# A two-group mixer layer on one core: m stored once as fp32 and split into two fp16 parts at the output projection

## The chip, the cores and the metric

One core of one Trainium2 chip. The metric is the device time of one execution in microseconds, lower is better.

## What is computed

One layer over 4096 prompt tokens and 8 x 16 sample tokens, width 1024:

```
h = rms_norm(x, norm_pre)
p = h @ w_in                      # 1024 x 3728: GLA, token-shifted RWKV and gate columns
o_gla  = gated linear attention (4 heads of 128), RMSNorm per head, * g_norm * silu(z_g)
o_rwkv = RWKV-7 delta rule (8 heads of 64), GroupNorm, + bonus, * silu(z_r)
m = concat([o_gla, o_rwkv])       # 512 + 512 columns per token
y = x + rms_norm(m @ w_out, norm_post)
```

The states and the last shifted row are outputs too. The matmuls with w_in and w_out need nearly fp32 precision: both factors are held as two fp16 parts (high and low), and three products are summed (high x high, low x high, high x low).

## The kernel before, in words

Tokens lie in 33 tiles of 128 (tile 0 holds the sample streams) and 17 blocks: block 0 is tile 0, blocks 1 to 16 have 256 tokens, two tiles each. There are two phases, one after the other, each with a program of its own for every engine.

**First phase, `gla_phase`.** A list of steps per block, `a_steps`, is run by all engines; each takes the steps that it has a function for. For each tile: `take_o` (ScalarE, L928) reads the outputs from PSUM, `squares` (TensorE) and `rnorm` (ScalarE) make the norm, `gate` (VectorE, L1111) multiplies by it (L1114) and by the gate (L1117). Then `high_m` (ScalarE, L948; the copy is L952) makes the fp16 high part in `m_hl`, `low_m` (VectorE, L1120; the subtraction is L1122) the low part, and `put_mg` (SP, L556; the store is L560) writes both to the scratch tensor `mg` in HBM. `take_o` of the next tile waits for `low_m`, since it overwrites `o_sb`. The last store and two others count into `tail_out`, for which the second phase waits.

**Second phase, `rwkv_phase`.** The order of each engine within a block is written out by hand: `PE_BODY`, `ACT_BODY`, `DVE_BODY`, `SP_BODY`. Names with `-` belong to the block before. The y of a tile is kept by `keep_y` in one of two slots of `yT`, normalised (`centred`, `deviation`, `normed`), scaled and shifted by `affine` (L2300), given the bonus (L2586) and gated (L2589) by `gated`. Then `high` (ScalarE, L2307), `low` (VectorE, L2593) and `put_m` (SP, L1639) split and store it as in the first phase, into the scratch tensor `mr`. `keep_y` of the tile two later waits for `low`.

**The output projection** has two sources of order. Per tile and half of w_out's columns TensorE runs 24 matmuls of 128x128 by 128x512 (`project_out`, all recorded at L1855), cut into six units of 4: 12 units a tile. In the bodies of the last two blocks and one more, where no more input projections are left, each of their places ("room") takes one unit: 108 units, 9 tiles. The other 24 tiles follow one after another, the tail. What the other engines do for a tile is put in a list with a due position in units (`out_jobs`); at a point `out` in the hand-written order an engine takes over all jobs that are due by then, and in the tail all in order of their positions. For tile t: `fetch` (SP) at 12t - 8, `o_squares` (ScalarE, L2326, Square with a sum) and `o_scaled` (VectorE, L2609) at 12t + 6 and 12t + 12, `o_sum` and `o_rstd` (L2331 to L2336) at 12t + 13, `o_done` (VectorE, L2624) at 12t + 15.6, `put_y` (SP, L1721) at 12t + 15.7.

`fetch` waits until tile t - 2 has been multiplied, loads the GLA half of m (L1709) and the RWKV half (L1711) into `m_c`, which has two slots, and x (L1714) into `x_c`, after the y of tile t - 2 has been stored from there. TensorE waits for the two m loads. For tile 0 `fetch` also loads norm_post. w_out comes in 16 parts of 128x512 (`get_ow`, SP, L1694), which `ow_high` (L2315) and `ow_low` (L2598) split; they are placed at points of blocks 14 and 15.

All queues are in order: an instruction that waits holds everything behind it on its engine.

Of the kernel before, what the change touches and what calls it, by code (L numbers as in the profile page):

```python
# [14 lines left out]

# [12 lines left out]
P = 128  # L28
# [36 lines left out]
def build(nc, t):  # L65
    with ExitStack() as ctx:
# [18 lines left out]
        c["d_full"] = Count(ctx.enter_context(nc.semaphore("r_d_full")), "d_full", 1, len(ROUND_NO))  # L85
        setup(nc, t, c)
# [105 lines left out]
def a_steps(b):  # L192
# [64 lines left out]
    if b == LAST:  # L257
# [15 lines left out]
        def own_mean(i):  # L273
            steps.extend((j, own[i]) for j in ("squares", "rnorm", "gate", "high_m", "low_m", "put_mg"))
# [23 lines left out]
        steps.extend((j, own[1]) for j in ("high_m", "low_m", "put_mg"))  # L298
# [52 lines left out]
def gla_phase(nc, t, c):  # L351
# [8 lines left out]
    with ExitStack() as ctx:  # L360
# [51 lines left out]
        m_hl = sb("m_hl", [P, 2, 4, P], F16)  # L412
# [86 lines left out]
        mh_ok = sig("m_high", 1, NT)  # L499
        ml_ok = sig("m_low", 1, NT)  # L500
# [24 lines left out]
        def _(sp):  # L525
# [30 lines left out]
            def put_mg(tile):  # L556
                b, i = home_of(tile)
# [254 lines left out]
        def _(act):  # L812
# [134 lines left out]

            def high_m(tile):  # L948
                act.wait_ge(m_ok.sem, m_ok.at(tile, 2))
                if tile:  # L950
                    act.wait_ge(mg_out.sem, mg_out.at(tile - 1, 1))
                act.activation(m_hl[:, 0], o_sb[:, :, :], ACT.Copy).then_inc(*mh_ok.up(tile))  # L952
# [9 lines left out]
            def split_w2(n):  # L962
# [7 lines left out]
                    "rnorm": rnorm, "high_m": high_m, "split_w2": split_w2,  # L970
# [13 lines left out]
        def _(dve):  # L984
# [126 lines left out]
            def gate(tile):  # L1111
                b, i = home_of(tile)
                dve.wait_ge(r_ok.sem, r_ok.at(tile, 2))
                dve.scalar_tensor_tensor(out=o_sb[:, :, :], in0=o_sb[:, :, :], scalar=g_norm[:, 0:1],  # L1114
                                         in1=o_sq[:, :, :], op0=ALU.mult, op1=ALU.mult).then_inc(*m_ok.up(tile))
                dve.wait_ge(m_ok.sem, m_ok.at(tile, 1))
                dve.tensor_tensor(o_sb[:, :, :], o_sb[:, :, :], zg[:, b % 2, :, columns(tile)],  # L1117
                                  ALU.mult).then_inc(*m_ok.up(tile))

            def low_m(tile):  # L1120
                dve.wait_ge(mh_ok.sem, mh_ok.at(tile, 1))
                dve.tensor_tensor(m_hl[:, 1], o_sb[:, :, :], m_hl[:, 0], ALU.subtract).then_inc(*ml_ok.up(tile))  # L1122
# [14 lines left out]
            def split_w2(n):  # L1137
# [9 lines left out]
                    "gate": gate, "low_m": low_m, "split_w2": split_w2,  # L1147
# [47 lines left out]
    join_e:2 affine:0 squares:2 out gamma taken:x0 odd:2 turned:3 high:0 rnorm:0 out rnorm:1 z1:3 join_e:3  # L1195
    keep_y:2 taken:x2 centred:1 out taken:x8 odd:3 turned:4 out deviation:1 affine:1 z1:4 join_e:4 keep_y:3
    high:1 out
""".split()
DVE_BODY = """
    zc:0 masked:1 -mixed:x10 -low:1 even:0 keep_w:1 mixed:x12 -bonus:0 out -r -bonus:1 next:0 join_o:1 mixed:x4  # L1200
    out masked:2 zc:1 decay out even:1 keep_w:2 normed:0 next:1 mixed:x6 join_o:2 gated:0 out masked:3 zc:2
    clamp:0 even:2 mixed:x0 keep_w:3 clamp:1 low:0 out unit:0 unit:1 next:2 join_o:3 k_prime mixed:x2 out
# [12 lines left out]
POST = ("centre", "variance", "centred", "deviation", "high", "normed", "affine", "gated", "low", "get_gate", "put_m")  # L1215
OUT_FROM = LAST - 1
OW_FROM = -6
OW_AT = [0, 0, 1, 1, 2, 2, 3, 3, 4, 4, 4, 5, 5, 5, 6, 6]
# [61 lines left out]

def out_jobs():
# [6 lines left out]
    for tile in range(NT):  # L1288
        p = 12.0 * tile
        put(max(p - 8.0, 0.0), "fetch", tile)  # L1290
# [21 lines left out]
def pe_program():  # L1312
# [3 lines left out]
    for part in [opening_jobs(PE_BODY)] + [body_jobs(PE_BODY, b) for b in range(NB + 1)]:  # L1316
        jobs = []
        for job, arg in part:
            if job == "room":
                jobs.append(("out", next(units)))  # L1320
# [10 lines left out]
def side_program(table, mine):  # L1331
# [4 lines left out]
    for b in range(NB + 1):  # L1336
        jobs = []
        for job, arg in body_jobs(table, b):
# [9 lines left out]
            for j, at in (("get_ow", OW_FROM), ("ow_high", OW_FROM + 1), ("ow_low", OW_FROM + 1)):  # L1348
                if j in mine:
                    jobs += [(j, k) for k in range(2 * KT) if OW_AT[k] + at == arg]  # L1350
            if "fetch" not in mine:
# [29 lines left out]
def rwkv_phase(nc, t, c):  # L1381
# [9 lines left out]
    mr_d = nc.dram_tensor("scratch_mr", (NT, P, 2, 4, P), F16, kind="Internal").ap()  # L1391
# [3 lines left out]
    with ExitStack() as ctx:  # L1395
# [55 lines left out]
        m_hl = sb("m_hl", [P, 2, 4, P], F16)  # L1451
# [20 lines left out]
        def Ss(j):  # L1472
# [5 lines left out]
                  m_hl[:, :, :, :].rearrange("p w g t -> p (w g t)").bitcast(F32))]  # L1478
# [8 lines left out]
        o_junk = [xb[:, 2 * h:2 * h + 2].rearrange("p c g t -> p (c g t)") for h in range(2)]  # L1487
# [47 lines left out]
        mr_out = sig("mr_out", 1, NT, 16)  # L1535
# [6 lines left out]
        ss_in = sig("ss_in", 8, 1, 16)  # L1542
# [4 lines left out]
        mc_in = [sig("mc_in0", 2, 17, 16), sig("mc_in1", 2, 16, 16)]  # L1547
# [5 lines left out]
        set_ok = sig("pool_set", SET_ALL, 1)  # L1553
# [20 lines left out]
        ones_ok = sig("ones", 1, 1)  # L1574
# [34 lines left out]
        mh_ok = sig("m_high", 1, NT)  # L1609
        ml_ok = sig("m_low", 1, NT)  # L1610
# [15 lines left out]
        def _(sp):  # L1626
# [75 lines left out]
            def fetch(tile):  # L1702
                b, i = home_of(tile)
                slot, n = tile % 2, tile // 2
                if tile == 0:
                    sp.wait_ge(y_full.sem, y_full.at(last_chunk(LAST - 2), 1))
                if tile >= 2:
# [996 lines left out]
```

## Time and profile before

| | us |
|---|---|
| median of 3 runs | 2375.19 (2369.25 to 2376.35) |
| span of the profiled execution, first to last instruction | 2370.8 |
| TensorE matmul busy | 2287.6 (96%) |
| ScalarE busy | 1427.8 (60%) |
| VectorE busy | 1308.5 (55%) |
| GpSimd busy | 569.9 (24%) |
| granted TensorE clock, mean | 0.994 |

The page gives the profiled execution's span and no time of its own around it; the span lies 4.4 us under the median of the runs. PE is TensorE, PEld its weight load, ACT ScalarE, DVE VectorE, POOL GpSimd, SP SyncE, of which only the issue of transfers is shown (SPq). A releaser is what an engine's idle time ended with. Matmuls are pipelined, so their durations overlap. PEclk is the granted clock as a share of full speed.

### The profile page before, as it was taken

How to read it: one execution, taken by the hardware profiler on the slowest of the kernel's cores; microseconds unless marked ns; L12 is line 12 of the kernel's file. 1: busy time of each engine (PE TensorE's matmuls, PEld its weight loads, DVE VectorE, ACT ScalarE, POOL GpSimd, SP SyncE). 2: the span in 40 equal slices, each digit the busy share in tenths (PEclk: the TensorE clock that was granted, in tenths of full speed). 3: DMA queues.
4: the chain of work that ended last, by engine and by line, in shares of the span. 5: the costliest groups of instructions: out<-in, count | busy, mean ns of one | idle time of the engine just before them, and what ended most of it. 6: DMA issues, size and time to landing. Idle time of an engine off the chain costs nothing. (4 is left out here: it accounts for less than half of the span.)

```text
span 2370.8 us, 72009 instructions
## 1 busy us (share of the span) xinstructions
PE 2287.6 (96%) x31129; PEld 1721.6 (73%) x31129; DVE 1308.5 (55%) x2477; ACT 1427.8 (60%) x2820; POOL 569.9 (24%) x1070
## 2 busy tenths in 40 slices
PE   6999999999999998889999999999999998999998
PEld 5777777777777766778888887888888874544443
DVE  6444444444444443566777776767777775432222
ACT  8466666666666645546776666666676774543323
POOL 0000000000000001155555554455555555000000
PEclk9999999999999998999999999999999999999999
DMA  7112222222211111123222222222222234354453
GB/s 244 67 55 73 73 73 69 69 81 91 73 54 54 54 63 48 43 52 78 76 71 73 69 67 76 76 76 76 76 67 74 56 93 145 115 167 150 152 160 125
DMA packets 198779, 204.74 MB, mean 86 GB/s; under 512 B 108608, under 2 KB 151936, under 8 KB 194112
## 3 DMA queue, kind: packets, MB, share of 16 engines
q1 hardware_dynamic: 196304, 184.41, 26.3%
q10 hardware_dynamic: 2160, 15.73, 1.8%
q8 instruction: 247, 4.05, 0.7%
q14 instruction: 68, 0.56, 0.1%
HBM read 119.81 MB, written 80.28 MB: 84 GB/s over the span
## 5 line engine op out<-in xcount | busy, mean ns | idle before, releaser
L675 PE MATMUL d<-h,w_hi 128*128 128x256 f16 (+1 forms) x3264 | 527.4, 270 | 9.8 <-DVE w_lo L1133 8.1
L675 PE MATMUL d<-h,w_lo 128*128 128x256 f16 (+1 forms) x1632 | 436.7, 270 | 0.0
L1816 POOL TENSOR_TENSOR r_inv_tmp<-r_inv 64x30 f32<-64x30 f32 (+14 forms) x480 | 259.5, 541 | 435.0 <-DMA r_inv<-scratch_blocks 398.7
L675 PEld LDWEIGHTS d<-h,w_hi 128*128 128x128 f16 x3264 | 315.1, 98 | 55.6 <-issue 14.9
L1855 PE MATMUL r_d<-h,w_hi 128*128 128x256 f16 (+1 forms) x1824 | 297.0, 269 | 0.8 <-DVE carry_s L2394 0.8
L1818 POOL TENSOR_TENSOR r_inv<-r_inv,r_inv_tmp 64x30 f32<-64x30 f32 (+14 forms) x480 | 278.2, 580 | 37.6
L1855 PE MATMUL first<-h,w_hi 128*128 128x256 f16 x1664 | 282.5, 273 | 0.0
L1855 PE MATMUL r_d<-h,w_lo 128*128 128x256 f16 (+1 forms) x912 | 241.6, 269 | 0.0
L1855 PE MATMUL first<-h,w_lo 128*128 128x256 f16 x832 | 227.2, 273 | 0.1
L1759 POOL MEMSET r_run_s<- 128x128 f16 x1 | 0.2, 204 | 930.6 <-POOLq L360 930.6
L1855 PEld LDWEIGHTS r_d<-h,w_hi 128*128 128x128 f16 x1824 | 171.9, 98 | 37.2 <-issue 14.7
L1855 PEld LDWEIGHTS first<-h,w_hi 128*128 128x128 f16 x1664 | 159.2, 98 | 33.9 <-issue 12.9
L675 PEld LDWEIGHTS d<-h,w_lo 128*128 128x128 f16 x1632 | 160.4, 98 | 17.5
L1855 PE MATMUL r_d<-w_hi,r_ops 128*128 128x512 f16 x560 | 167.0, 379 | 0.2 <-DMA r_ops<-scratch_mr 0.2
L675 PE MATMUL d<-w_hi,h 128*128 128x512 f16 x528 | 157.0, 379 | 2.0 <-DVE w_lo L1133 2.0
L1855 PE MATMUL first<-w_hi,r_ops 128*128 128x512 f16 x496 | 148.1, 380 | 0.0
L2168 ACT ACTIVATE r_praw<-r_carry 128x2 f32<-128x2 f32 (+1 forms) x112 | 22.5, 201 | 155.3 <-PE r_d L1855 77.5
L1855 PE MATMUL r_d<-w_lo,r_ops 128*128 128x512 f16 x280 | 106.2, 379 | 0.0
L1855 PEld LDWEIGHTS r_d<-w_hi,r_ops 128*128 128x128 f16 x560 | 53.9, 98 | 64.7 <-issue 1.5
L1114 DVE SCALAR_TENSOR_TENSOR o_sb<-o_sb,g_norm,o_sq 128x512 f32<-128x512 f32 x33 | 24.8, 751 | 137.4 <-ACT o_sq L946 137.4
L675 PE MATMUL d<-w_lo,h 128*128 128x512 f16 x264 | 100.1, 379 | 0.0
L1855 PEld LDWEIGHTS r_d<-h,w_lo 128*128 128x128 f16 x912 | 89.7, 98 | 10.0 <-issue 1.0
(323 smaller groups left out, 4792.3 us busy)
## 6 DMA issues: line engine op xcount, KB each, us to landing
h<-in_x SPq DMA_DIRECT2D x33, 512.0 KB, 3.8
r_ops<-in_x SPq DMA_DIRECT2D x33, 512.0 KB, 4.2
out_y<-r_ops SPq DMA_DIRECT2D x33, 512.0 KB, 2.9
scratch_hT<-h SPq DMA_DIRECT2D x16, 1024.0 KB, 7.0
h<-scratch_hT ACTq DMA_DIRECT2D x15, 1024.0 KB, 7.0
scratch_mg<-m_hl SPq DMA_DIRECT2D x33, 256.0 KB, 2.0
r_zr<-scratch_zr SPq DMA_DIRECT2D x33, 256.0 KB, 3.6
r_bon<-scratch_bonus SPq DMA_DIRECT2D x33, 256.0 KB, 4.7
```

The source lines that it names most:

```text
L675: mm = pe.matmul(out, lhs(k, a, w), rhs(k, a, w), start=(n == 0), stop=(n == len(terms) - 1))
L1114: dve.scalar_tensor_tensor(out=o_sb[:, :, :], in0=o_sb[:, :, :], scalar=g_norm[:, 0:1], in1=o_sq[:, :, :], op0=ALU.mult, op1=ALU.mult).the ...
L1759: pool.memset(m[:, :], v).then_inc(*set_ok.up(0))
L1816: step(pool.tensor_tensor(tmp, inv[0:n, 0:u, u:u + 1].to_broadcast([n, u, w]), inv[0:n, u:u + 1, u + 1:32].to_broadcast([n, u, w]), ALU.mult))
L1818: step(pool.tensor_tensor(inv[0:n, 0:u, u + 1:32], inv[0:n, 0:u, u + 1:32], tmp, ALU.add))
L1855: mm = pe.matmul(out, lhs(k, a, w), rhs(k, a, w), start=(m == 0), stop=(m == 3 * KT - 1))
L2168: act.activation(praw[:, x % 2, 0:ng, 0], carry[:, g0:g0 + ng], ACT.Copy)
```

## The change

m of both groups is stored once, as fp32, in the new scratch tensor `m_d`. `high_m`, `low_m`, `high` and `low` and their places in the orders go. Instead the output projection loads both halves of a tile as fp32 (`get_m`) into one buffer each, `m_fp`: `m_f`, in the place of `m_hl`, and `up`, free after the last low-rank product; ScalarE copies both to fp16 (`m_high`), and VectorE subtracts (`m_low`), into `m_c`. TensorE waits for `m_low`. `m_fp` has one slot: `get_m` of a tile waits for `m_low` of the tile before. `get_m(0)` has a point of its own, four points before the projection begins. Some semaphores are merged or renamed to make room.

```diff
-            steps.extend((j, back[i]) for j in ("squares", "rnorm", "gate", "high_m", "low_m", "put_mg"))
+            steps.extend((j, back[i]) for j in ("squares", "rnorm", "gate", "put_mg"))
...
             def put_mg(tile):
-                sp.wait_ge(ml_ok.sem, ml_ok.at(tile, 1))
+                sp.wait_ge(m_ok.sem, m_ok.at(tile, 2))
-                sp.dma_start(t["mg"][b][:, i], m_hl[:, :, :, :]).then_inc(*stored)
+                sp.dma_start(c["m_d"][tile][:, 0], o_sb[:, :, :]).then_inc(*stored)
...
             def take_o(tile):
-                    act.wait_ge(ml_ok.sem, ml_ok.at(tile - 1, 1))
+                    act.wait_ge(mg_out.sem, mg_out.at(tile - 1, 1))
...
+M_FROM = -4
...
     for tile in range(NT):
         p = 12.0 * tile
+        if tile:
+            put(p - 8.0, "get_m", tile)
+        put(max(p - 5.0, 0.0), "m_high", tile)
+        put(max(p - 5.0, 0.0), "m_low", tile)
         put(max(p - 8.0, 0.0), "fetch", tile)
...
             def put_m(tile):
-                sp.wait_ge(ml_ok.sem, ml_ok.at(tile, 1))
-                sp.dma_start(mr_d[tile], m_hl[:, :, :, :]).then_inc(*mr_out.up(tile))
+                sp.wait_ge(post_ok.sem, post_ok.at(tile, 7))
+                sp.dma_start(m_d[tile][:, 1], yT[:, tile % 2]).then_inc(*mr_out[tile % 2].up(tile // 2))
...
+            def get_m(tile):
+                if tile:
+                    sp.wait_ge(ml_ok.sem, ml_ok.at(tile - 1, 2))
+                else:
+                    sp.wait_ge(d_full.sem, d_full.at(ROUND_NO[LAST, "la2"], 1))
+                sp.dma_start(m_fp[0], m_d[tile][:, 0]).then_inc(*ss_in.up(8 + 2 * tile))
+                sp.wait_ge(mr_out[tile % 2].sem, mr_out[tile % 2].at(tile // 2, 1))
+                sp.dma_start(m_fp[1], m_d[tile][:, 1]).then_inc(*ss_in.up(9 + 2 * tile))
...
-                if tile >= 2:
-                    sp.wait_ge(d_full.sem, d_full.at(ROUND_NO["out", tile - 2, 1], 1))
-                sp.dma_start(m_c[:, slot, 0], t["mg"][b][:, i]).then_inc(*mc_in[slot].up(n))
-                sp.wait_ge(mr_out.sem, mr_out.at(tile, 1))
-                sp.dma_start(m_c[:, slot, 1], mr_d[tile]).then_inc(*mc_in[slot].up(n))
...
             def project_out(arg):
-                    pe.wait_ge(mc_in[tile % 2].sem, mc_in[tile % 2].at(tile // 2, 2))
+                    pe.wait_ge(ml_ok.sem, ml_ok.at(tile, 2))
...
             def keep_y(q):
-                    act.wait_ge(ml_ok.sem, ml_ok.at(tile - 2, 1))
+                    act.wait_ge(mr_out[tile % 2].sem, mr_out[tile % 2].at(tile // 2 - 1, 1))
...
+            def m_high(tile):
+                if tile == 0:
+                    act.wait_ge(y_full.sem, y_full.at(last_chunk(LAST - 2), 1))
+                if tile >= 2:
+                    act.wait_ge(d_full.sem, d_full.at(ROUND_NO["out", tile - 2, 1], 1))
+                act.wait_ge(ss_in.sem, ss_in.at(8 + 2 * tile + 1, 1))
+                for a in range(2):
+                    act.activation(m_c[:, tile % 2, a, 0], m_fp[a], ACT.Copy).then_inc(*mh_ok.up(tile))
...
             def out_squares(arg):
+                if h:
+                    act.wait_ge(os_ok.sem, os_ok.at(tile, 1))
-                act.activation(o_junk[h], bank_of(("out", tile, h))[:, :], ACT.Square,
+                act.activation(o_junk, bank_of(("out", tile, h))[:, :], ACT.Square,
...
+            def m_low(tile):
+                for a in range(2):
+                    dve.wait_ge(mh_ok.sem, mh_ok.at(tile, a + 1))
+                    dve.tensor_tensor(m_c[:, tile % 2, a, 1], m_fp[a], m_c[:, tile % 2, a, 0],
+                                      ALU.subtract).then_inc(*ml_ok.up(tile))
```

## Rows read from the trace of the kernel before

**Rows 1.** The page, busy time, share of the span and instructions
```profile
PE 2287.6 (96%) x31129; PEld 1721.6 (73%) x31129; DVE 1308.5 (55%) x2477; ACT 1427.8 (60%) x2820; POOL 569.9 (24%) x1070
```

**Rows 2.** Busy time by stretch: stretch, length, engines, PEclk, DMA share, GB/s
```profile
110.00:936.00 826.00, 818.78 (x6943) 633.71 (x6940) 369.76 (x715) 516.17 (x831) 0.00 (x0) 1.00 0.20 65
...
1100.00:1950.00 850.00, 840.74 (x17456) 698.24 (x17455) 624.42 (x1154) 592.29 (x1317) 453.43 (x816) 1.00 0.28 73
1950.00:2080.00 130.00, 115.93 (x2035) 68.96 (x2034) 68.65 (x131) 65.47 (x150) 34.96 (x61) 0.99 0.44 132
...
2125.00:2365.00 240.00, 237.87 (x1103) 107.63 (x1100) 66.63 (x117) 76.38 (x165) 0.00 (x0) 1.00 0.47 147
```

**Rows 3.** The chain in order of time, first and last whole tile: start, us, engine
```profile
2103.87 10.36 PE first L1855 x48
...
2352.51 10.37 PE first L1855 x48
```

**Rows 4.** Timeline of the first phase's end, by engine; last row: page, issues
```profile
910.88 0.38 ACT L936 ACTIVATE o_sq<-OB 128x256 f32<-128x256 f32 x1 [0.84 <-DVE m_hl L1122]
...
926.72 1.10 PE L788 MATMUL d<-o_sq,ones_dv 128*128 128x512 f32 x2 [1.67 <-ACT o_sb L937]
...
935.08 0.32 SPq L560 DMA_DIRECT2D scratch_mg<-m_hl  x1
...
scratch_mg<-m_hl SPq DMA_DIRECT2D x33, 256.0 KB, 2.0
```

**Rows 5.** Lines L2307 and L2593: ns min/median/max; idle of L2307 until
```profile
L2307 ACT ACTIVATE r_m_hl<-r_yT x33: 613/631/634, 1112.2 to 2096.1; 128x512 f16<-128x512 f32 x33
...
  DVE r_yT L2589: 23.0, 16
...
L2593 DVE TENSOR_TENSOR r_m_hl<-r_yT,r_m_hl x33: 677/691/908, 1112.9 to 2097.5; 128x512 f16<-128x512 f32 x33
```

**Rows 6.** Timeline where w_out is loaded, SP, ACT and PE
```profile
1962.44 1.42 SPq L1694 DMA_DIRECT2D h<-in_w_out  x3
...
1969.93 1.97 ACT L2315 ACTIVATE w_hi<-h 128x512 f16<-128x512 f32 x3 [5.27 <-DMA h<-in_w_out]
...
1976.34 0.46 PE L2033 MATMUL r_EO<-r_S,r_ops 64*64 64x64 f32 x16 [3.65 <-DVE r_S L2557]
```

**Rows 7.** Busy time by stretch, around the same place; last row: timeline, PE
```profile
1965.00:1970.00 5.00, 4.83 (x93) 3.08 (x94) 0.69 (x1) 0.07 (x1) 4.29 (x10) 1.00 1.00 325
...
1975.00:1980.00 5.00, 3.66 (x51) 2.05 (x52) 4.69 (x9) 3.44 (x7) 4.53 (x7) 0.77 0.67 159
...
1990.00:2000.00 10.00, 7.74 (x137) 4.20 (x130) 6.71 (x12) 4.77 (x12) 8.67 (x18) 1.00 0.13 49
...
1999.62 0.43 PE L1978 MATMUL r_EO<-r_TD,h 64*64 64x32 f32 x16 [2.26 <-DVE r_Zc L2530]
```

**Rows 8.** Tiles 6 to 8: timeline of DVE, ACT, SP, and the chain
```profile
2080.68 0.69 DVE L2589 TENSOR_TENSOR r_yT<-r_yT,r_zr 128x512 f32<-128x512 f32 x1
...
2082.18 5.29 PE r_d L1855 x24
...
2091.54 1.65 ACT L2300 ACTIVATE r_yT<-r_yT,lnb_s,sc 128x128 f32<-128x128 f32 x4 [0.76 <-DVE r_yT L2580]
...
2097.64 0.34 SPq L1721 DMA_DIRECT2D out_y<-r_ops  x1
```

**Rows 9.** Timeline of a tail tile, PE and SP
```profile
2196.95 0.59 PE L1855 MATMUL r_d<-w_hi,r_ops 128*128 128x512 f16 x2
...
2202.10 0.72 SPq L1711 DMA_DIRECT2D r_ops<-scratch_mr  x1
```

**Rows 10.** Tail loads of m: issue of L1709, ns min/median/max; landing of L1711
```profile
L1709 SPq DMA_DIRECT2D r_ops<-scratch_mg x24: 320/432/1477, 2108.4 to 2346.7; - x24
...
DMA to landing us min/median/max: 3.6/3.9/4.5
```

**Rows 11.** Timeline, three copies to fp16 in a row on ACT
```profile
1957.85 1.66 ACT L2315 ACTIVATE w_hi<-h 128x512 f16<-128x512 f32 x3
```

More of the change, by code:

```diff
@@ L16 @@
+import itertools
 from contextlib import ExitStack
@@ L273, in own_mean @@
         def own_mean(i):
-            steps.extend((j, own[i]) for j in ("squares", "rnorm", "gate", "high_m", "low_m", "put_mg"))
+            steps.extend((j, own[i]) for j in ("squares", "rnorm", "gate", "put_mg"))
         steps += [("get_h", 0), ("get_h", 1)]
@@ L297, in a_steps @@
         steps.append(("put_zr", b))
-        steps.extend((j, own[1]) for j in ("high_m", "low_m", "put_mg"))
+        steps.append(("put_mg", own[1]))
         return steps
@@ L1194 @@
     out tanh:la0 squares:0 tanh:lw2 tanh:la2 deviation:0 odd:1 out turned:2 k_factor taken:x6 z1:2 keep_y:1
[L1195 removed]
+    join_e:2 affine:0 squares:2 out gamma taken:x0 odd:2 turned:3 rnorm:0 out rnorm:1 z1:3 join_e:3
     keep_y:2 taken:x2 centred:1 out taken:x8 odd:3 turned:4 out deviation:1 affine:1 z1:4 join_e:4 keep_y:3
[L1197 removed]
+    out
 """.split()
 DVE_BODY = """
[L1200 removed]
+    zc:0 masked:1 -mixed:x10 even:0 keep_w:1 mixed:x12 -bonus:0 out -r -bonus:1 next:0 join_o:1 mixed:x4
     out masked:2 zc:1 decay out even:1 keep_w:2 normed:0 next:1 mixed:x6 join_o:2 gated:0 out masked:3 zc:2
[L1202 removed]
+    clamp:0 even:2 mixed:x0 keep_w:3 clamp:1 out unit:0 unit:1 next:2 join_o:3 k_prime mixed:x2 out
     -td masked:4 zc:3 beta a mixed:x8 strict:0 out strict:1 even:3 keep_w:4 normed:1 rkk next:3 join_o:4 gated:1
@@ L1214 @@
 AHEAD = ("scores", "inner", "turn", "solve", "join", "masked", "keep_w", "join_o", "turned", "z1", "join_e")
-POST = ("centre", "variance", "centred", "deviation", "high", "normed", "affine", "gated", "low", "get_gate", "put_m")
+POST = ("centre", "variance", "centred", "deviation", "normed", "affine", "gated", "get_gate", "put_m")
 OUT_FROM = LAST - 1
 OW_FROM = -6
+M_FROM = -4
 OW_AT = [0, 0, 1, 1, 2, 2, 3, 3, 4, 4, 4, 5, 5, 5, 6, 6]
@@ L1319, in pe_program @@
             if job == "room":
-                jobs.append(("out", next(units)))
+                jobs += [("out", u) for u in itertools.islice(units, 1)]
             elif job == "piece":
@@ L1350, in side_program @@
                     jobs += [(j, k) for k in range(2 * KT) if OW_AT[k] + at == arg]
+            if "get_m" in mine and arg == M_FROM:
+                jobs.append(("get_m", 0))
             if "fetch" not in mine:
@@ L1450, in rwkv_phase @@
         bon = sb("bon", [P, 4, P])
-        m_hl = sb("m_hl", [P, 2, 4, P], F16)
+        m_f = sb("m_f", [P, 4, P])
         st = sb("st", [P, 2, 4])
@@ L1486, in rwkv_phase @@
         npost = hT[:, LAST % 2].rearrange("p a k t -> p (a k t)")[:, 0:2 * D].bitcast(F32)
-        o_junk = [xb[:, 2 * h:2 * h + 2].rearrange("p c g t -> p (c g t)") for h in range(2)]
+        m_fp = [m_f[:, :, :], up[:, :].rearrange("p (g t) -> p g t", g=4)]
+        o_junk = lor[:, :].bitcast(BF16)
         wv_hi = w_hi[:, :].rearrange("p (k n) -> p k n", k=KT)
@@ L1608, in rwkv_phase @@
         post_ok = sig("post", 7, NT)
-        mh_ok = sig("m_high", 1, NT)
-        ml_ok = sig("m_low", 1, NT)
+        mh_ok = sig("m_high", 2, NT)
+        ml_ok = sig("m_low", 2, NT)
         ow_hi = sig("ow_high", 2 * KT, 1)
@@ L1833, in _, with released @@
             RELEASE.update({r: (carry_ok, k + 1) for k, r in enumerate(XROUNDS)})
+            def released(old):
+                if old[0] == "out":
+                    pe.wait_ge(ot_ok.sem, ot_ok.at(old[1], old[2] + 1))
+                elif old[0] == "centre":
+                    pe.wait_ge(yc_ok.sem, yc_ok.at(old[1], 2 * old[2] + 2))
+                elif old[0] == "variance":
+                    pe.wait_ge(post_ok.sem, post_ok.at(old[1], 1))
+                else:
+                    s, k = RELEASE[old[1]]
+                    pe.wait_ge(s.sem, s.at(old[0], k))
             def claim(key):
@@ L2319, in out_squares @@
                 act.wait_ge(d_full.sem, d_full.at(ROUND_NO["out", tile, h], 1))
-                if tile == 0 and h == 0:
-                    act.wait_ge(x_out.sem, x_out.at(LAST, 4))
                 if tile:
@@ L2339, in _ @@
                     "gamma": gamma, "load_h": lambda b: load_h(b + 2), "centred": centred, "deviation": deviation,
-                    "high": high_part, "affine": affine, "k_factor": k_factor, "ow_high": split_out, "o_squares": out_squares, "o_rstd": out_rstd,
+                    "m_high": m_high, "affine": affine, "k_factor": k_factor, "ow_high": split_out, "o_squares": out_squares, "o_rstd": out_rstd,
                     "odd": odd_unknowns, "keep_y": keep_y, "turned": keep_turned, "z1": keep_z1,
@@ L2627, in _ @@
             does = {"mixed": mixed, "decay": decay, "clamp": clamp, "unit": unit, "k_prime": k_prime, "rkk": rkk, "kappa": make_kappa, "r": make_r, "beta": make_beta, "a": make_a, "strict": strict,
-                    "bonus": bonuses, "normed": normed, "gated": gated, "low": low_part, "ow_low": split_out,
+                    "bonus": bonuses, "normed": normed, "gated": gated, "m_low": m_low, "ow_low": split_out,
                     "o_scaled": out_scaled, "o_sum": out_sum, "o_done": out_done, "zc": add_state,
```

75 lines of the change are left out of this document (23 added, 52 removed).

## The prediction, made before the changed kernel was run

> **What bounds the kernel now.** I read the page's busy times first: TensorE is busy for 2287.6 of 2370.8 us [rows 1]. The table of stretches says where the other 83 us lie: 7 in the first head group (110 to 936), 9 in the body of the second (1100 to 1950), 14 between 1950 and 2080, 2 in the tail; the rest is the start of either group, where the change moves nothing [rows 2]. The chain of waits ends in 25 links of 10.36 us, 48 matmuls each, from tile 8 (2103.87) to tile 32, with no other engine between them [rows 3]. So a freed operation of ScalarE or VectorE is worth at most the few idle us of its stretch, while every us by which a tail tile is late adds its full length. The sum is made against the span of 2370.8; the median of the runs shown is 2375.2, 4.4 more, and that distance is carried over.
>
> **First head group.** Per tile one copy on ScalarE and one subtraction on VectorE go (33 of each; their twins of the second group took 631 and 691 ns [rows 5]). SP stores the fp32 tile as soon as it is gated: as many bytes in rows as long. In exchange take_o now waits for the store to have landed, no longer for the subtraction. In the usual order four or five rounds lie between the two, so that costs nothing; only in the last block are they close. There the old wait ended at 910.88 [rows 4]; the gated tile is ready 1.4 us earlier, its store lands 2.0 us after issue [rows 4], so take_o comes 0.6 us later. Behind it on ScalarE are a table load and a tanh, and TensorE has a round to do meanwhile: nothing. For the last tile the order is friendlier: tanh of zr no longer stands behind a copy, and TensorE's wait of 1.67 us on o_sb shrinks by about 0.35 [rows 4]. At the hand-over SP issued the last store at 935.08, after the subtraction [rows 4]; without it the phase ends about 0.25 earlier. **Together -0.6** (bounds -1.2 and +0.5, the latter if take_o's 0.6 isn't covered).
>
> **Body of the second group.** Again one copy and one subtraction per tile go; the copy also held ScalarE for 1.4 us in 16 blocks, waiting for the gated tile [rows 5]. TensorE idles only 9.3 us in those 850 [rows 2], so the relief is worth between nothing and 3: **-1.0**. keep_y waits for the landed store two tiles back; that store now goes out right after get_gate's two loads, more than 10 us ahead: nothing. The new semaphores and the waits of o_squares on its own engine are order that the engine keeps anyway.
>
> **Where w_out is loaded.** SP issued tile 0's two m loads, x and norm_post, and behind them three parts of w_out at 1962.44; ScalarE waited 5.27 us for the part that it splits at 1969.93, and TensorE behind it 3.65 us for the state at 1976.34 [rows 6]. The DMA engines were full, at 325 GB/s [rows 7]. get_m(0) moves 30 us forward, past these on SP's queue: it stands between two jobs with idle time around it and takes two issues of 0.43 to 0.72 us [rows 9, 10]. So 0.52 MB leave a full queue: 1.6 us at 325 GB/s, 1.8 with the earlier issue. Against it m_low(0) puts 1.3 us of VectorE ahead of the masks and the state, which makes TensorE's next product late by about 1.2; this only moves into the 3.65 us wait behind it. The wait also cost clock: 0.77 of full speed in 1975 to 1980, where a wait of 2.26 us, in 1990 to 2000, left it at 1.00 [rows 7]. If the wait halves, some of that comes back; I take 0.8 of the 0.23 x 5 = 1.15 us. **Together -2.6** (bounds -5, both vanish; 0, the delay eats the gain).
>
> **Tiles 1 to 8 of the projection**, which lie between the last blocks. I placed each new job by its due time (loads 8 units ahead, the split 5; a unit is 4 matmuls). For tiles 1 to 5 the loads land and the split ends 1 to 5 us before TensorE gets there. Tile 6: VectorE comes to its subtractions after the gated tile (from 2080.68, 0.69 long), ends at about 2082.8, while TensorE began the tile at 2082.18 [rows 8]: **+0.6**. Tile 7 is just in time, but ScalarE and VectorE stand in its split until about 2093.8, in front of the last normalisation. So the affine step of 1.65 us, at 2091.54 before, comes at 2094.5, o_squares behind it about 2 us late, the y store of tile 6, at 2097.64 before [rows 8], about 2.6 late, and the loads of tile 8 stand behind that store: they land at 2105.0, the split ends at 2107.1, and TensorE wants it at 2104.5: **+2.6** (bounds 0 and 4).
>
> **The tail.** For one tile [rows 9]: TensorE starts it at 2196.95; the end of the tile before goes through Square, rstd and o_done to the y store; right behind it SP issues the m loads of the next tile, the second at 2202.10, 5.15 after the start. Landing takes 3.9 us in the median (3.6 to 4.5) [rows 10]: 9.05. The next tile starts at 10.36, so 1.3 us are spare. That place on SP stays the same: get_m stands at 12t - 8, put_y of two tiles before at 12t - 8.3. The x load follows as before. Now comes the split between landing and matmul. Copies follow each other at 0.52 ((1.66 - 0.63)/2 [rows 11, 5]), so the second ends 1.15 after the first's start; its subtraction takes 0.69; three hand-overs of 0.04 and a weight load of 0.1 make it **2.1 us against 1.3 spare: 0.8 late**. (Bounds: 1.8 for the split and 3.6 for landing give 0.2 late; 4.5 gives 1.4.) Readiness hangs on the end of the tile two before, not on the last. So when one tile waits 0.8, the next finds its data in time, and the one after waits again: a wait at every second tile, of the larger lateness of the pair, about 0.95. From tile 10 to 32 these are 12: **+11.4** (4 to 18). ScalarE's and VectorE's other tail work is not pushed: the split is over 0.1 us before o_squares is due. What is saved in TensorE's own work: nothing, the matmuls are the same.
>
> There is a lower price for a load in the Trainium skill, DMA: Bandwidth & Descriptors, whose section on the anatomy of one DMA fits 2.0 us and the bytes at 436 GB/s, for GpSimd's path; that would be 2.6 us for 256 KB, land the loads 1.3 earlier and leave no tail wait. The trace disagrees: no such load of the tail landed under 3.6 [rows 10], since a 512 KB store is issued ahead of it.
>
> **Sum**: -0.6 - 1.0 - 2.6 + 0.6 + 2.6 + 11.4 = **+10.4**: span 2381, time **2385.6**. What a measurement here can tell from no change is 0.3%, 7.1 us.
>
> **Rivals.**
> 1. The tail hides the split. It needs landing plus split in 5.2 us instead of 6.0: a load that lands in 3.1. For it: 1.3 us are spare, and the wait grows only from there. Against: the shortest landing is 3.6. It would leave -0.6 - 1.0 - 2.6 + 0.6 + 2.6, or with tile 8 hidden too -3.6: 2372 to 2374. 0.2, with the half way cases between this and mine.
> 2. Faster: the w_out stretch holds more than I give it. If the load's absence takes away the whole 3.65 and the clock's 1.15, and the body gives 3, with a hidden tail, it is 2375.2 - 0.6 - 3 - 4.8 = 2366.8. Both halves must come out; it decides at a tail lateness under 0.1. 0.06.
> 3. The tail's waits feed themselves: from 0.9 late on, m_high of one tile stands on ScalarE in front of o_squares of the tile before, its y store and thus the next loads come later. Each second wait then grows to 1.5 and the others no longer vanish: 18 to 22 in the tail instead of 11.4, 2392 to 2396. SP needed up to 1.48 instead of 0.43 us to issue a load [rows 10], which speaks for it; typical tiles stay 0.1 below. 0.14.
> 4. The waits cost clock, as in 1975 to 1980: 1.15 us at each of 12, 14 more, 2399. A wait of 2.26 us left the clock whole [rows 7], so 0.03. The Trainium skill, TensorE: Matmul & The Clock Gate, Part 1, says "the default state is throttled, and activity releases the throttle"; by that rule alone idle time is dangerous, and the long wait agrees, the short one doesn't show it.
>
> **How the numbers follow.** My case has 0.57, its own range being 2379 to 2392. The range 2375 to 2394 leaves out rival 2, rival 4, part of 1 and the top of 3. Slower by over 0.3% (above 2382.3): most of my case, rivals 3 and 4: 0.66. Within 0.3%: the low end of my case and most of rival 1: 0.27. Faster: 0.07.
>
> **What would show it.** In the changed profile: waits of TensorE on the subtraction of m_low at every second tail tile, near 0.8 to 1.0; links of 10.36 broken by them; the ScalarE copy idle on DMA m_f or up before it; SP's loads still behind the y store. One wait of 2 to 3 us at tile 8. ScalarE's wait for w_out near 3.5 and TensorE's on the state near 2, the clock above 0.77 there. SP's last store of the first group near 934.5, not 935.08. Wrong if the tail shows no waits, if they come at every tile, or if a block before 1950 loses TensorE time.

## The result, and the profile after

The changed kernel takes 2381.0 us (median of 18 runs, 2375.2 to 2387.7), the kernel before beside it 2372.0 (18 runs): a ratio of 1.0037, 95% interval 1.0027 to 1.0047. That is 8.8 us more, where the prediction had 10.4. (The ratios here are those on record; the quotient of the two medians can differ from them by up to 0.0006.) Applied to the 2375.2 on which the prediction stood, the ratio gives 2384.0, forecast 2385.6. The profiled execution has a span of 2380.2 us, 9.4 more than before.

The busy times by stretch, in the columns of [rows 2] (stretch, length, then PE, PEld, DVE, ACT, POOL, the granted clock, DMA share, GB/s):

```profile
110.00:936.00 826.00, 818.33 (x6923) 633.76 (x6951) 348.38 (x685) 496.83 (x801) 0.78 (x3) 1.00 0.20 66
1100.00:1950.00 850.00, 842.40 (x17520) 700.47 (x17518) 613.04 (x1137) 580.73 (x1297) 446.13 (x817) 1.00 0.28 74
1950.00:2080.00 130.00, 119.11 (x2027) 69.56 (x2026) 75.66 (x139) 72.54 (x165) 36.25 (x61) 0.97 0.44 132
2125.00:2365.00 240.00, 230.06 (x1058) 102.37 (x1057) 91.92 (x156) 96.48 (x198) 0.00 (x0) 1.00 0.46 145
```

Against [rows 2] TensorE is busier in the third stretch and idles 10 us in the last, where it idled 2. What it waits for from 2130 on (line, releaser, us in total, times, longest):

```profile
PE r_d L1858 <- DVE r_ops L2600: 8.4, 11, 1.1
PE first L1858 <- DVE r_ops L2600: 1.5, 1, 1.5
```

L2600 is the subtraction of m_low. These are twelve waits, at tile 11, at every second tile from there to tile 31, and at tile 32; tile 10 ahead of them waits 0.63. In the chain of waits (start, us, engine and line) the unbroken links of 10.36 [rows 3] are gone. Between the start of one tile that waited and that of the tile two behind it the chain now reads:

```profile
2198.36 10.54 PE r_d L1858 x48
2208.92 0.69 ACT r_lor L2332 x2
2209.62 1.28 ACT L2337
...
2211.57 1.43 DVE r_ops L2632 x2
2213.01 0.34 SPq L1722
...
2213.40 0.43 SPq L1702
...
2213.87 3.96 DMA up<-scratch_m
2217.87 0.04 issue
2217.91 0.64 ACT r_ops L2313
2218.58 0.55 DVE r_ops L2600
...
2219.19 0.70 DVE r_ops L2600
2219.89 0.14 issue
2220.02 10.54 PE r_d L1858 x48
```

The reader is to see the loop: the first tile's end, Square (L2332), rstd, o_done (L2632), the y store (L1722), behind it on SP the m loads (L1702), 3.96 us until they land, the split, and the tile after next. It closes in 2220.02 - 2198.36 = 21.66 us. Two tiles of TensorE's own work take 20.72, so 0.94 falls to each pair, as forecast (0.95): some 0.75 of waiting and 0.18 by which the link of the tile that waited is longer (10.54).

The longest wait, 1.51 us at tile 32, is not part of this pattern: it follows directly on a tile that waited. The second load of that tile took 5.57 us to land, where those of the tiles before it took 3.7 to 4.7:

```profile
2354.32 5.57 DMA up<-scratch_m
...
2362.08 10.53 PE first L1858 x48
```

Two other profiles with the loads in this place (the second buffer and tile 8 alone first, below) have no wait at tile 32.

The tiles ahead of the tail, TensorE's starts with the wait in brackets:

```profile
2076.36 0.59 PE L1858 MATMUL r_d<-w_hi,r_ops 128*128 128x512 f16 x2 [0.54 <-DVE r_ops L2600]
...
2100.72 0.59 PE L1858 MATMUL first<-w_hi,r_ops 128*128 128x512 f16 x2 [2.63 <-DVE r_ops L2600]
```

Tile 6 and tile 8 wait 0.54 and 2.63 (forecast 0.6 and 2.6).

To see the rest I compared start times of the same instructions. Profiles of one kernel differ by a few us in places, so the kernel before was profiled three times, and beside the changed kernel stand the experiments (described below) that have the stretch in question unchanged. Chunks are the 64-token steps of the recurrence, counted from 0. The table, in us:

| stretch | before | changed | difference | forecast |
|---|---|---|---|---|
| end of the first group, take_o of tile 29 to that of tile 32 | 50.0, 50.1, 50.0 | 46.2 or 46.3 in eight profiles, 44.7 in two | -3.8 (-5.3 in two) | -0.6 |
| from the second group's first product to its first product with the state | 93.5, 97.3, 96.0 | 96.0 to 98.0, mean 97.4 of ten | +1.8 | 0 |
| body, state product of chunk 0 to chunk 57 | 908.1, 903.3, 907.3 | 898.1 to 904.0, mean 901.4 of nine | -4.9 | -1.0 |
| w_out, chunk 57 to 61 | 71.2, 72.5, 69.6 | 67.1 to 70.4, mean 68.5 of seven | -2.6 | -2.6 |
| chunk 61 to the end of the last tile, which holds the waits of tiles 6 to 32 | 352.0, 351.8, 351.9 | 367.8 (its own profile) | +15.9 | +14.6 |

The first row is the surprise: it repeats to 0.1 us, and it is six times what was forecast. The reason stands in ScalarE's timeline. Before the change:

```profile
884.87 0.63 ACT L946 ACTIVATE o_sq<-o_sq 128x512 f32<-128x512 f32 x1
887.05 0.63 ACT L952 ACTIVATE m_hl<-o_sb 128x512 f16<-128x512 f32 x1 [1.55 <-DVE o_sb L1117]
887.70 1.28 ACT L884 ACT_TABLE_LOAD   x1
...
893.04 0.55 PE L753 MATMUL OB<-q_sb,Sd 64*128 64x128 f32 x1 [4.00 <-ACT k_tok L926]
```

and after it:

```profile
887.20 0.63 ACT L944 ACTIVATE o_sq<-o_sq 128x512 f32<-128x512 f32 x1
887.85 1.28 ACT L882 ACT_TABLE_LOAD   x1
...
893.20 0.34 PE L751 MATMUL OB<-q_sb,Sd 64*128 64x128 f32 x1 [1.82 <-ACT k_tok L924]
```

The copy `high_m` of tile 29 (L952) stood in the last block between that tile's rstd (L946) and the block's decay exponentials, which begin with the table load (L884). It waited 1.55 us for the gated tile and took 0.63: 2.18 us, by exactly which TensorE's wait on k_tok went from 4.00 to 1.82. The rest of the 3.8 is clock. TensorE's busy time and the granted clock (the column after the number of instructions) before, and after:

```profile
890.00:895.00 5.00, 1.96 (x11) 0.73 0.00 0
895.00:900.00 5.00, 5.00 (x31) 0.59 0.00 0
```

```profile
890.00:895.00 5.00, 3.18 (x22) 0.93 0.14 52
895.00:900.00 5.00, 5.00 (x37) 0.73 0.02 3
```

Before, (0.27 + 0.41) x 5 = 3.4 us of full clock are missing in the two slices, some 0.4 of it while TensorE still waited; afterwards (0.07 + 0.27) x 5 = 1.7. From the product that ended the wait (893.04 and 893.20) to take_o of tile 32 it took 32.32 us before and 30.77 after, so that 1.55 us came back behind the 2.18. In the two profiles with 44.7 the clock stayed at 1.00 throughout. Ahead of this place the copies were worth nothing: from take_o of tile 1 to that of tile 29 every profile of either kind takes the same 750 us to 0.1.

The second row of the table goes with the clock and not with the kernel. TensorE's busy time and granted clock, the kernel before in its first profile and in its second:

```profile
955.00:965.00 10.00, 6.52 (x122) 1.00 0.23 57
1005.00:1015.00 10.00, 6.93 (x160) 1.00 0.63 180
```

```profile
955.00:965.00 10.00, 6.53 (x95) 0.66 0.08 13
1005.00:1015.00 10.00, 6.93 (x156) 0.88 0.48 101
```

The first took 93.5 us, the second 97.3. The changed kernel has 1.00 and 0.66 there and took 96.2, the one with the early loads (first of the experiments) 0.66 and 0.83, and 97.8. Whether the change has a part in when the clock falls there is not shown.

The timelines at the other two places that the prediction named, the end of the first group (PE, SP) and the load of w_out (ACT), in the changed kernel:

```profile
925.32 1.10 PE L786 MATMUL d<-o_sq,ones_dv 128*128 128x512 f32 x2 [1.33 <-ACT o_sb L935]
...
933.45 0.43 SPq L558 DMA_DIRECT2D scratch_m<-o_sb  x1
...
1963.64 1.94 ACT L2321 ACTIVATE w_hi<-h 128x512 f16<-128x512 f32 x3 [0.81 <-DMA h<-in_w_out]
```

Against [rows 4, 6] the wait on o_sb is 0.34 shorter, the last store is issued 1.6 us earlier (933.45 for 935.08), and ScalarE's 5.27 us for w_out are 0.81. That last wait scatters: it is 3.4 to 5.3 us in the three profiles of the kernel before, and 0.55 to 3.0 in the nine with the w_out parts in their changed place and nothing added.

### The profile page after: what moved, and what is told of

It reads as the page before. It is cut to its first block and busy times, and to the rows that moved or that the text cites. A ratio compares the mean times of both kernels' runs of the same rounds, so it can differ in the third digit from the quotient of the medians.

```text
span 2380.2 us, 71977 instructions
## 1 busy us (share of the span) xinstructions
PE 2289.9 (96%) x31098; PEld 1722.2 (72%) x31129; DVE 1308.9 (55%) x2477; ACT 1426.0 (60%) x2820; POOL 562.3 (24%) x1070
```

## The experiments

**Loads of m ahead of the y store.** For the m loads of every tile, in out_jobs:

```diff
-            put(p - 8.0, "get_m", tile)
+            put(p - 8.5, "get_m", tile)
```

> The loads of m of a tile go on SP's queue ahead of the y store of the tile two before (due position 12t - 8.5 in place of 12t - 8); nothing else. My theory (the tail is late because the loads stand behind that store, 5.15 us after the tile's start, and the split follows them): the loads leave about 8 us earlier, so the 12 waits of the tail and the wait of 2.6 us at tile 8 go, 0.54 at tile 6 stays. That is 14 us less than the changed kernel: 0.998 of the kernel before. Rival, the split itself (two copies and two subtractions between load and matmul) or the single fp32 buffer sets the pace: the waits stay, 1.004. Rival, the waits cost nothing because the tail has other slack: 1.004 too.

2366.0 us, 0.9976 [0.9966, 0.9986] of the kernel before: by the ratios 5.7 us faster than it and 14.5 faster than the changed kernel (by the medians side by side 4.6 faster than the kernel before). The waits from tile 6 to 32 are a single one of 0.5 us (tile 6), where there were 15 of 13.8 in all, and the links are whole again:

```profile
PE r_d L1858 <- DVE r_ops L2600: 0.5, 1, 0.5
```

```profile
2209.70 10.36 PE r_d L1858 x48
2220.05 10.36 PE first L1858 x48
```

The first load of m of the tile that TensorE starts at 2220.05 now leaves here:

```profile
2207.19 0.32 SPq L1702 DMA_DIRECT2D r_m_f<-scratch_m  x1
```

That is 12.9 us ahead of its tile, where the changed kernel had 6.6 (2213.40 and 2220.02 in the chain above), so it leaves 6.2 us earlier and not the 8 that were expected. It goes out as soon as the last subtraction of the tile before has ended (2207.17): in this place the single buffer does set its time, at no cost.

So the tail's loss is the place of the loads on SP's queue, not the split as such. This version is faster than both kernels.

**The wait in two halves.** TensorE asks for the first half of the split at unit 0 of a tile and for the second at unit 3:

```diff
-                if n == 0:
-                    pe.wait_ge(ml_ok.sem, ml_ok.at(tile, 2))
+                if n in (0, 3):
+                    pe.wait_ge(ml_ok.sem, ml_ok.at(tile, 1 if n == 0 else 2))
```

> TensorE waits for the first subtraction of a tile before its first matmul and for the second one only before the fourth unit (the RWKV half of m is used from the 13th matmul on). The second subtraction ends 0.6 us after the first. My theory: lateness falls from about 0.85 to 0.25, so the 12 tail waits add up to about 3 instead of 10 us and tile 6's wait of 0.54 goes: 8 us less than the changed kernel, 1.000 to 1.001 of the kernel before. Rival, the waits come from a clock or a dispatch effect and not from the length of the split: nothing changes, 1.004.

2372.8 us, 1.0008 [0.9994, 1.0021]. In the tail the waits shrink to

```profile
PE r_d L1858 <- DVE r_ops L2600: 1.9, 5, 0.9
```

from 9.9 us in 12: one copy and subtraction less in front of TensorE is worth nearly the whole lateness. The wait at tile 8 stays (2.57 us), since there the load was late.

**A second buffer, same place on the queue.** From tile 11 on odd tiles load into memory of their own, so that get_m need not wait for the last subtraction of the tile before:

```diff
+        m_g = TT[:, 0].rearrange("p c g t -> p (c g t)")
...
-                if tile:
-                    sp.wait_ge(ml_ok.sem, ml_ok.at(tile - 1, 2))
+                if tile == 11:
+                    sp.wait_ge(u_full.sem, u_full.at(NQ - 1, 1))
+                elif tile:
+                    sp.wait_ge(ml_ok.sem, ml_ok.at(tile - (2 if tile > 11 else 1), 2))
```

> From tile 11 on odd tiles load m into a second pair of fp32 buffers, so get_m waits for the split of the tile two before, not of the last one; its place on SP behind the y store stays. My theory (SP's place sets the load's time, not the buffer): no change, waits at every second tail tile of 0.6 to 1.1 us, 1.004 of the kernel before. Rival, the single buffer: the waits go, 0.999 to 1.000.

2377.9 us, 1.0025 [1.0015, 1.0036], overlapping the changed kernel's interval. The tail's waits are the same:

```profile
PE r_d L1866 <- DVE r_ops L2608: 8.7, 11, 1.1
```

With the loads behind the y store, the one buffer is not what makes them late.

**Copies twice.** From tile 9 on ScalarE makes each copy of the split twice, the second behind the first:

```diff
                 for a in range(2):
+                    if tile > 8:
+                        act.activation(m_c[:, tile % 2, a, 0], m_fp[a], ACT.Copy).then_inc(*once_ok.up(tile - 9))
+                        act.wait_ge(once_ok.sem, once_ok.at(tile - 9, a + 1))
```

> The changed kernel (1.0037), with each of ScalarE's two copies of the split done twice, one after the other, for tiles 9 to 32: the split, 2.1 us so far, gets about 1.4 us longer. My theory (a tile waits at every second place for landing plus split minus the spare time): TensorE's wait goes from 0.95 to about 2.4 us per pair of tiles, 12 x 1.4 = 17 us in the tail, ratio 1.011. Rival 3 of the prediction, which begins where the copies come to stand in front of the Square of the tile before: that Square, its y store and the next loads come up to 1 us later, the second tile of the pair waits too, and the tail grows by 24 us or more, ratio 1.014 or over.

2399.0 us, 1.0114 [1.0098, 1.0131], 18 us over the changed kernel; 17 were expected by the simple sum. The pattern looks different:

```profile
2185.90 0.59 PE L1859 MATMUL r_d<-w_hi,r_ops 128*128 128x512 f16 x2 [1.24 <-DVE r_ops L2604]
...
2197.03 0.59 PE L1859 MATMUL first<-w_hi,r_ops 128*128 128x512 f16 x2 [0.61 <-DVE r_ops L2604]
...
2208.74 0.59 PE L1859 MATMUL r_d<-w_hi,r_ops 128*128 128x512 f16 x2 [1.20 <-DVE r_ops L2604]
...
2219.90 0.59 PE L1859 MATMUL first<-w_hi,r_ops 128*128 128x512 f16 x2 [0.63 <-DVE r_ops L2604]
```

Both tiles of a pair wait, 1.2 and 0.6 us. On ScalarE (its copies, then the Square of the tile before):

```profile
2205.40 0.63 ACT L2315 ACTIVATE r_ops<-r_m_f 128x512 f16<-128x512 f32 x1 [2.31 <-DMA up<-scratch_m]
...
2207.24 0.63 ACT L2317 ACTIVATE r_ops<-up 128x512 f16<-128x512 f32 x1
2207.78 0.58 ACT L2336 ACTIVATE r_lor<-first 128x512 bf16<-128x512 f32 x1
```

The Square at 2207.78 comes straight behind the last copy, with no idle time: it was held, as in rival 3. But its tile ended at 2197.03 + 10.53 = 2207.56, so it was held for 0.2 us only, and the pair doesn't show it. A pair takes 2208.74 - 2185.90 = 22.84 us, 1.18 more than the 21.66 of the changed kernel, and the split has grown by as much (from landing to the end of the second subtraction 3.3 us for 2.1). The Square that this pair's loop goes through wasn't held: it starts at 2196.46, 0.3 us after ScalarE was free. The second tile's wait is mostly the same lateness too: its data are ready 12.4 us after the end of the tile two before it, 0.2 of that by the hold, and the tile between covers 1.24 of waiting and 10.53 of work, which leaves 0.6. Twelve pairs at 1.18 make 14 us; the profile's tail is 16.3 longer than the changed kernel's, and 1.7 us of that is full clock missing after a wait of 2.35 us at 2138.49 (granted clock 0.90 and 0.75 in 2135 to 2145). So the simple sum holds up to this length of the split, and the 24 us or more of that rival do not come.

**Tile 7 alone first, tile 8 alone first.** The same edit of the place, for one tile each:

```diff
-            put(p - 8.0, "get_m", tile)
+            put(p - (8.5 if tile == 7 else 8.0), "get_m", tile)
```

> The changed kernel with one edit: the m loads of tile 7 alone are issued ahead of the y store of tile 5 instead of behind it. My theory for tile 8 (its split waits behind that of tile 7, the affine step and the y store of tile 6): the split of tile 7 ends earlier, the affine step is no longer pushed, and TensorE's wait at tile 8 falls from 2.63 us to about 0.9, what a tail tile waits anyway; the tail's 0.95 per two tiles stays. Rival: the wait at tile 8 comes from the load of tile 8 itself behind its own y store; then it stays at 2.6.

The wait at tile 8 fell to 2.06 us, not to 0.9: this expectation failed. ScalarE's first copy for tile 7 started straight behind the last normalisation's two operations, no longer waiting for the load, and was only 0.5 us earlier for it. What pushes the affine step is mostly the split's own time in front of it, not the lateness of its load.

> The changed kernel with the m loads of tile 8 alone ahead of the y store of tile 6. With the loads of tile 7 early, TensorE's wait at tile 8 only fell from 2.63 to 2.06 us. Theory now: what makes tile 8 late is the place of its own loads behind a y store that hangs on the affine step; which of its causes delays that step is secondary. Then the wait at tile 8 is gone here (0 to 0.3 us), and the tail's waits stay as in the changed kernel. Rival: the split of tile 8 itself stands behind the last normalisation on ScalarE and VectorE, so that a wait of 1 us or more is left at tile 8.

With `tile == 8` in that edit the wait at tile 8 is gone. The waits from tile 6 on are

```profile
PE r_d L1858 <- DVE r_ops L2600: 9.6, 13, 1.0
```

0.54 at tile 6 and twelve in the tail, from tile 9 on. So the loads' place behind the y store of tile 6 decides at tile 8 as in the tail. There is one profile of each; their times, 2377.8 and 2379.2, tell nothing apart.

**More in the queue where w_out is loaded.** A load of 512 KB that nobody needs, ahead of x of tile 0, as many bytes as the change takes out:

```diff
+                    sp.dma_start(x_c[:, 1, :], t["x"][1]).then_inc(*np_in.up(0))
```

> Just ahead of tile 0's x load, where the kernel before loaded m, SP issues one more load of 512 KB (x of tile 1, loaded again later), so that the parts of w_out stand behind as many bytes as before the change. My theory of the w_out stretch: ScalarE waits for w_out again as long as before (5 us), TensorE waits for the state 2 us more, and the product that meets the state of chunk 61 comes at 2007 or later where the changed kernel had 2004.8: 2 to 3 us more in the span up to there. Rival, the stretch got shorter because the copies and subtractions of the last blocks went away: no change there.

This expectation failed. ScalarE's wait for w_out is 2.9 us and not 5, which the kernel with the copies twice shows too (3.0), without that load. TensorE's wait on the state stays at 0.2, where the kernel before has 3.65, 3.0 and 2.1 in its three profiles and the other changed kernels 0.3 at most. Chunks 57 to 61 take 70.5 us against a mean of 68.5, and the kernel with the copies twice takes 70.4. So in this one profile the bytes in the queue do not bring the wait back, and the reason that the prediction gave for this stretch is not confirmed. The other candidate, the copies and subtractions of the last blocks that are gone, was not tried: the two runs that put old work back stop at tile 25.

**w_out ahead of x and norm_post**, on top of the early loads:

```diff
-            if "fetch" in mine:
-                jobs += late
             for j, at in (("get_ow", OW_FROM), ("ow_high", OW_FROM + 1), ("ow_low", OW_FROM + 1)):
...
-            if "fetch" not in mine:
-                jobs += late
+            jobs += late
```

> The kernel with the early loads (0.9976), and on SP's queue the parts of w_out due at a point go ahead of the x tile and norm_post due at the same point (1 MB that nobody needs before tile 0 ends). If full DMA queues in front of the w_out parts still cost TensorE time, ScalarE's wait of 2.0 us for a part goes and the stretch from 1940 to 2005 us gets 1 to 2 us shorter: 0.9970. Rival: what TensorE waits for there (2.9 us twice) hangs on the recurrence and not on w_out; then no change, 0.9976.

2365.6 us, 0.9981 [0.9967, 0.9995]: no change. ScalarE no longer waits for w_out at all, and TensorE waits in 1935 to 2015 as in the changed kernel (4.2 and 2.9 there):

```profile
PE r_EO L1978 <- DVE r_Zc L2533: 4.0, 2, 3.3
PE r_EO L1978 <- DVE h L2501: 2.8, 1, 2.8
```

What is left there hangs on the recurrence.

**The old work put back.** On top of the early loads, the second group's copy and subtraction at their old places into a spare buffer (tiles 0 to 25), then those of the first group too (all 33):

```diff
+            def high_again(tile):
+                if tile < 26:
+                    act.wait_ge(post_ok.sem, post_ok.at(tile, 7))
...
+                    act.activation(again[:, 0], yT[:, tile % 2], ACT.Copy).then_inc(*again_ok.up(tile))
```

> On top of the kernel with the early loads (0.9976 of the kernel before): the copy on ScalarE and the subtraction on VectorE of the second head group are put back at their old places for tiles 0 to 25, writing to a buffer that nobody reads; storing, loading and the tail stay as changed. The prediction gave this work 1.0 us in the body: 0.9980, the stretch between the first and the last state product before 1940 us grows by about 1. Rival: the body's relief is the part of the gain that I put too low, 3 to 5 us: 0.999 or over, TensorE's idle time in 1100 to 1935 rises from 3.4 us (mean of five profiles) back toward the 7.2 of the kernel before, and the stretch from 899 to 903 us back toward 908.

> As the run before, and the copy and subtraction of the first head group are put back too (all 33 tiles, with the wait of take_o on the subtraction; the store waits for it as before). The prediction gave both groups together 1.6 us: 0.9983. Rival with a body relief of 3 to 5 us: 0.9993 to 1.000. In either case the end of the first phase should fall back by 0.3 to 1.4 us, to near 938.0 for the first state products after it, where the changed kernel had 936.6.

The first gives 2366.6 us, 0.9984 [0.9974, 0.9994], both together 2369.2, 0.9996 [0.9985, 1.0007]. Against 0.9976 that is 1.9 and 4.7 us. The first interval holds both my 0.9980 and the rival's 0.999 and tells nothing apart; the second leaves out my 0.9983 and holds the rival's 0.9993 to 1.000. The body took 902.9 us in the first (mean without: 901.4) and 911.4 in the second, though the two kernels have the same body: it scatters by more than the effect. The first group does not scatter: with its copies back TensorE's wait on k_tok is back at its old length,

```profile
PE OB L754 <- ACT k_tok L927: 4.0, 1, 4.0
```

and its end takes 48.7 us instead of 46.2, which is 2.5 where 0.3 to 1.4 were expected (50.0 before, with more of the clock lost: here 0.77 and 0.89 in 895 to 905, 1.7 us of full clock). So the old work is what made the wait.

**The kernel before, twice more.**

> The kernel before, unchanged, for a second profile. If the body's relief of 5 to 10 us between the first and the last state product before 1940 us, which seven profiles without the copies show against one profile of the kernel before, is real, that stretch takes 908 us here too, and TensorE idles about 7 us in 1100 to 1935. If it is the scatter of one execution, the stretch takes 899 to 905 us, and idle time is near 3.4.

> The kernel before, unchanged, for a third profile, with the same expectations as the one ahead of it: 908 us and 7 us idle if the relief is real, 899 to 905 us and 3.4 if it is scatter. The first phase should end near 938.0 us in both, against a mean of 935.4 without the copies, if the 2.6 us there are real.

The body takes 903.3 and 907.3 us, TensorE idles 4.9 and 8.2 us in 1100 to 1935. One fits scatter, one the relief; with the first profile the mean is 906.3, 4.9 over the mean of the nine, and one of the three lies inside the range of the nine. The second group's first product starts at 938.7 and 938.6, as in the first profile (938.0), and at 934.1 to 937.0 in the ten with the first group changed. These are times from the start of the program, and the first group itself begins up to 3 us apart (take_o of tile 1 at 125.3 to 128.7), so the distances in the table are the better measure.

## Why the prediction was right, point by point

- **The tail** (+11.4): right in place, cause and size. 0.94 per pair in the chain, the loads behind the y store; moving them ahead removes it, a second buffer does not. The waits stand at tiles 10 and 11, at every second tile to 31, and at tile 32. The last, 1.51 us, was not in the sum and comes from one load that landed late (5.57 us).
- **One reason in it was wrong.** I put the 3.6 to 4.5 us of landing [rows 10] down to the 512 KB store issued ahead. With the loads ahead of that store they still took 3.0 to 4.1 (first, median 3.3 against 3.7) and 3.4 to 5.4 us (second, median 3.7 against 3.9). That no such load of the tail landed under 3.6 holds for the second loads; the first ones did from 3.5 on. The fit in the Trainium skill, DMA: Bandwidth & Descriptors, section on the anatomy of one DMA, which is for GpSimd's path and would give an estimate of 2.6 us, does not hold for these loads in either place (3.0 at least). The early place gains by starting 6.2 us sooner, and at most 0.4 by landing faster.
- **Tile 6 and tile 8** (+0.6, +2.6): measured 0.54 and 2.63. The chain to tile 8 was right in its last part (loads behind the y store, the y store behind the affine step); moving tile 7's loads gave back 0.57 of it, so its part about what pushes the affine step was wrong: the split's own time, not a late load.
- **First group** (-0.6): this step failed. It measured -3.8, and -2.5 with the copies put back and the same loss of clock. I looked at the wait on o_sb (1.67 [rows 4], now 1.33, the 0.35 forecast) and at the last store, and gave VectorE's and ScalarE's relief nothing else. The larger wait stood 33 us earlier, TensorE's 4.00 us on k_tok in the last block, and it was not in my rows. The copy waited 1.55 us there on its own account, so its removal was worth 2.18, and 1.55 us of clock came with it. take_o does wait for the store's landing now, as said (3.65 us at 910.45), and nothing waits for it.
- **Behind the hand-over** the second group's start gave back about 1.8 us of the gain, which I had at nothing. It goes with the granted clock at 955 to 965 and 1005 to 1015: the kernel before spans 93.5 to 97.3 us there by itself, and is back at 93.8, with a clock of 1.00 in both, in the run with both groups' copies. Why the clock falls more often with the first group changed is open.
- **The body** (-1.0, bounds 0 and 3): by the profiles -4.9, with a scatter of 5 to 6 us in either kernel. The medians of the early-load kernel are the other scale: it is 4.6 (medians side by side) to 5.7 us (ratio, interval 3.3 to 8.1) faster than the kernel before, 0.5 more without tile 6, for everything outside the tail, where I had 4.2. Of that the first group and the start of the second hold about 2.0 net and w_out 2.6, so that 0.5 to 1.6 are left for the body. So my 1.0 may have been too small, but neither scale decides it.
- **w_out** (-2.6): -2.6 on the mean, in part by luck. ScalarE's wait, which I had at 3.5, is 0.81 (0.55 to 3.0 over the profiles), and TensorE's wait of 3.65 us on the state, which I had at 2, is gone. Putting the bytes back did not bring it back, so that my reason for it is not shown. Of the clock nothing came back: 0.73 in 1960 to 1965 after the change, where 0.77 stood in 1975 to 1980 [rows 7], and 0.84 and 0.82 in 1990 to 2000, where it was 1.00. And the waits on Z and h in 1935 to 2015 grew from 5.2 to 7.1 us in all, the next limit.
- **The sum**: +10.4 forecast, 8.8 measured. The gains were larger than I had them, 5.1 to 6.2 us by the medians (9.5 by the means of the table) for 4.2. The loss from tile 6 on was 15.9 by the start times, 1.3 over the 14.6 forecast, about what tile 32's late load cost; the run with more in the queue, whose projection is the same, lost 13.5 there. So the tail carries the forecast by its mechanism, and that the rest came out near -4.2 is luck: -3.8 for -0.6, then 1.8 back for nothing.
- **Rivals.** 1 is out: in the changed kernel no second load of the tail landed under 3.7. 2 is out in the tail, though the gain that it asked of the stretches before was partly there, in the first group instead of the body and w_out. 3 is out for this split, and with 1.2 us more on the split the Square was held by 0.2 us without a price in the pair. 4 is out here: the clock stays at 1.00 in the tail with waits up to 1.5 us, and the links of tiles that waited are 10.54; waits over 2 us did cost clock in other runs (last section).

## What to carry to other kernels

Where work is moved from storing to loading, the load's place in its queue has to move with it. Here the load had 1.3 us to spare; the split needed 2.1, and a queue entry half a unit earlier was worth 14.5 us. And when an instruction leaves an engine, look for every wait of the bounding engine on that engine, the rare ones in the last block too: where the bounding engine waits on what stands behind it, an instruction that itself waited is worth its wait plus its length. Of the first group's copies those up to tile 28 were worth nothing, while the next one, of tile 29, was worth 2.2 us and clock.

## What the runs showed of the hardware

The clock price of one wait of TensorE differs between executions. After the 4.00 us wait the three profiles of the kernel before show 0.73 and 0.59, 0.81 and 0.51, 0.79 and 0.53 in the two slices of 5 us from 890 on (the lowest near the 1.2 GHz level), 3.4 us of full clock each. That is not fixed either: the kernel with both groups' copies put back waits the same 4.00 us and loses 1.7 (1.00, 0.77 and 0.89 from 890 to 905). After the same point with a wait of 1.82 us two profiles show 1.00 and 1.00, others 0.93 and 0.73 or 0.76 and 0.90. That alone moves the end of the group by 1.5 us, between 44.7 and 46.2. The same holds for TensorE's wait at tile 8: after 2.66 us (second buffer) the slices from 2095 on show 0.77 and 0.89, after 2.06 us (tile 7 first) 0.66 and 1.00, after 2.63 us in the changed kernel 1.00 and 1.00. The Trainium skill, TensorE: Matmul & The Clock Gate, Part 1, has the clock released by activity; the long wait agrees in all four profiles that have it, and after the short one the clock fell in eight profiles of ten.
